# Grouped attention scores of the last two layers: two 64-row float32 products a block replaced by four 128-row float32r products, and the query norm moved behind the scores

## The reference

```python
def gqa_axial_attention(q, k, v, qn_g, kn_g, tables):
    q = rmsnorm_2(q.reshape(b, s, H_B, HEAD_DIM), qn_g)      # 8 query heads of 64
    k = rmsnorm_2(k.reshape(b, s, KV_HEADS, HEAD_DIM), kn_g) # 2 key heads of 64
    q = apply_axial_rope(q, tables)
    k = apply_axial_rope(k, tables)
    scale = HEAD_DIM ** -0.5
    ...
        sc = jnp.einsum('bqkgd,bskd->bkgqs', qblk, k) * scale
        p = jax.nn.softmax(sc, axis=-1)
        return jnp.einsum('bkgqs,bskd->bqkgd', p, v)

for l in range(2):
    h = rmsnorm_2(x, pre_g[l])
    u_a, v_a, g_a, q, k, v, g_b = split(h @ w_in[l])
    y_a = gmlp_group(u_a, layernorm(v_a), ...) * silu(g_a)
    y_b = gqa_axial_attention(q, k, v, ...) * silu(g_b)
    x = x + rmsnorm_2(concat(y_a, y_b) @ w_out[l], post_g[l])
```

## Time and profile before

| | |
|---|---|
| profiled execution | 1713.68 us, of it the span 1711.9 us |
| runs | 1713.58, 1709.22, 1713.06 us (median 1713.06) |
| granted TensorE clock | 0.993 over the span |
| PE busy | 97% of the span |
| DVE, ACT, POOL busy | 50%, 43%, 41% |
| chain that ended last | PE 86%, DVE 7%, ACT 4%, issue 2% |
| layer 1 of the second block | about 1206 to 1460 us |
| layer 2 of the second block | about 1460 to 1712 us |

### The profile page before, as it was taken

How to read it: one execution, slowest core, us unless ns; L and a number is a source line. 1 busy time by engine, 2 the same in 40 slices (tenths; PEclk the granted TensorE clock), 3 DMA queues, 4 the chain that set the end, 5 groups by cost and what they waited for, 6 DMA issues and landing times.

```text
span 1711.9 us, 24057 instructions
## 1 busy us (share of the span) xinstructions
PE 1663.8 (97%) x8728; PEld 1283.7 (75%) x8728; DVE 849.4 (50%) x1352; ACT 744.7 (43%) x1177; POOL 706.1 (41%) x406
## 2 busy tenths in 40 slices
PE   7899899999999999999999999999999999999998
PEld 7555678888888876666788888888876668876666
DVE  6787546555431125334466666411446454556354
ACT  6433434444432325444455555433326643526541
POOL 4433243444455444443534444554424423434332
PEclk9999999999999999999999999999999999999999
DMA  7112132333333332111323333333421112311111
GB/s 253 57 50 63 50 99 74 98 98 98 98 108 101 103 94 74 50 51 37 100 85 98 98 98 97 107 103 99 129 62 50 51 61 64 124 53 52 60 50 62
DMA packets 40251, 143.77 MB, mean 84 GB/s; under 512 B 4592, under 2 KB 4592, under 8 KB 40176
## 3 DMA queue, kind: packets, MB, share of 16 engines
q1 hardware_dynamic: 39168, 139.59, 26.6%
q10 hardware_dynamic: 1008, 3.15, 0.6%
HBM read 140.62 MB, written 2.10 MB: 83 GB/s over the span
## 4 chain that ended last, share of the span: by engine, by line
PE 86%; DVE 7%; ACT 4%; issue 2%; DMA 0%; POOL 0%; DVEq 0%; SPq 0%; ACTq 0%; POOLq 0%
PE banks L1686 23%; PE banks L1688 22%; PE banks L1687 22%; PE banks L1899 3%; PE banks L1864 3%; PE banks L1882 2%; PE banks L1732 2%; PE banks L1734 2%; PE banks L1733 2%; PE banks L1952 1%; ACT prob L723 1%; DVE chain L1373 1%; DVE nmax L1204 1%; DVE xs_lo L1165 1%; PE banks L2172 1%
## 5 line engine op out<-in xcount | busy, mean ns | idle before, releaser
L579 POOL TENSOR_TENSOR w_lo<-raw,w_hi 128x1024 fp32r<-128x1024 f32 x252 | 610.2, 2430 | 763.1 <-ACT w_hi L662 762.8
L1686 PE MATMUL banks<-xs_hi,w_hi 128*128 128x512 f32 (+2 forms) x1488 | 600.0, 403 | 10.3 <-DVE xs_lo L1424 4.2
L1688 PE MATMUL banks<-xs_hi,w_lo 128*128 128x512 f32 (+2 forms) x1488 | 579.2, 389 | 0.0
L1687 PE MATMUL banks<-xs_lo,w_hi 128*128 128x512 f32 (+2 forms) x1488 | 578.7, 389 | 0.0
L662 ACT ACTIVATE w_hi<-raw 128x1024 fp32r<-128x1024 f32 x255 | 263.9, 1053 | 295.0 <-PE banks L1688 257.1
L1686 PEld LDWEIGHTS banks<-xs_hi,w_hi 128*128 128x128 f32 x1488 | 281.0, 189 | 83.4 <-issue 18.9
L1688 PEld LDWEIGHTS banks<-xs_hi,w_lo 128*128 128x128 f32 x1488 | 280.9, 189 | 58.9
L1687 PEld LDWEIGHTS banks<-xs_lo,w_hi 128*128 128x128 f32 x1488 | 281.6, 189 | 53.2 <-issue 2.9
L589 POOL TENSOR_SCALAR prob<-prob,rinv 128x512 f32<-128x512 f32 (+3 forms) x144 | 88.7, 628 | 184.8 <-DVE rinv L1213 184.5
L723 ACT ACTIVATE prob<-banks,nmax 128x512 f32<-128x512 f32 (+3 forms) x144 | 83.2, 582 | 170.5 <-DVE nmax L1204 170.3
L1687 PE MATMUL banks<-hid_lo,w_hi 128*128 128x512 f32 x352 | 136.9, 389 | 0.0
(11 more groups left out here) (250 smaller groups left out, 1900.5 us busy)
## 6 DMA issues: line engine op xcount, KB each, us to landing
raw<-wstream SPq DMA_DIRECT2D x255, 512.0 KB, 3.6
x<-xT SPq DMA_DIRECT2D x4, 512.0 KB, 10.1
out<-pt SPq DMA_DIRECT2D x8, 256.0 KB, 2.0
memx<-memT SPq DMA_DIRECT2D x2, 512.0 KB, 7.0
ws_sb<-wsT ACTq DMA_DIRECT2D x2, 512.0 KB, 4.4
qk<-post_rows ACTq DMA_DIRECT2D x2, 512.0 KB, 3.8
sb_sb<-sbT ACTq DMA_DIRECT2D x2, 256.0 KB, 5.1
rope_sb<-rope ACTq DMA_DIRECT2D x1, 512.0 KB, 6.9
```

Of the source, the lines that this page charges most:

```text
L579: nc.gpsimd.tensor_tensor(w_lo[s][:].rearrange("p k c -> p (k c)"), raw[s][:], w_hi[s][:].rearrange("p k c -> p (k c)").bitcast(f32), SUB) ...
L1686: MM(dst, w_hi[slot][:, k, :], hi, start=start, stop=False)
L1687: MM(dst, w_hi[slot][:, k, :], lo, start=False, stop=False)
L1688: return MM(dst, w_lo[slot][:, k, :], hi, start=False, stop=stop)
```

## The change

In both layers of the second block:

1. **Scores.** `q_stack` holds, for each head of a pair, the float32r rounding of the query on one half of the partitions and the remainder on the other half. `k_hi` holds the rounded key of a head on both halves, `k_lo` its remainder on both halves. Each head's scores are two 128-row float32r products, `q_stack` by `k_hi` and `q_stack` by `k_lo` (four for a block), in place of one 64-row float32 product a head.
2. **Splits.** ACT makes the rounded parts (`q_high`: two 64x512 copies a pair, at units 6, 10, 13, 16; `k_high`: four at unit 7). DVE makes the remainders (`q_low`: two 64x512 subtractions a pair, at the same units; `k_low`: four at unit 8).
3. **Norm.** Only the key tile is cast and multiplied (`key_cast`, `key_norm`, at unit 7). The roots of the queries stay in `head_r`, times 64^-0.5, and are used as row factors: as `scale` of the exponentials, and by two 128x1 products behind the maximum.
4. **Silu.** The tiles of `gb` are done two at a time at units 12 and 16, those of `ga` two at unit 20 and one at unit 21.
5. **Turning x.** `x_turn` uses two banks in turn.
6. **Tables.** `k_lo` lies on the rope table, which is therefore loaded again in layer 2 (512 KB).

```diff
@@ attention on ACT
+                    kw = {"scale": head_r[:, 2 * i + e:2 * i + e + 1]} if a.scale_rows else {}
                     A(prob[b % 2][:, e, 0:nk], a.s[b % len(a.s)][:, e, 0:nk], ACT.Exp, bias=nmax[:, n:n + 1],
-                      accum_out=rsum[:, n:n + 1]).then_inc(at_exp, 1)
+                      accum_out=rsum[:, n:n + 1], **kw).then_inc(at_exp, 1)
@@ layer loop on ACT
-                if l == 0:
-                    act.dma_start(rope_sb[:], rope).then_inc(l2_in, 16)
+                act.dma_start(rope_sb[:], rope).then_inc(l2_in, 16)
...
+                def q_high(p):
+                    act.wait_ge(rope_ok, 5 * l + p + 1)
+                    if p == 1:
+                        act.wait_ge(rope_ok, 5 * (l + 1))
+                        act.wait_ge(qk_lo, 12 * l + 2)
+                    if p >= 2:
+                        act.wait_ge(at_s, 2 * (a.i0 + QT * (p - 1)))
+                    for e in range(2):
+                        A(q_stack[p % 2][e][half(e), :], qk[half(e), p, :], ACT.Copy).then_inc(qk_hi, 1)
+
+                def k_high():
+                    act.wait_ge(cast_down, cast_no[f"qk{l}"] + 1)
+                    for e in range(2):
+                        for h in range(2):
+                            A(k_hi[half(h), e, :], qk[half(e), 4, :], ACT.Copy).then_inc(qk_hi, 1)
...
+                    if j == 6:
+                        q_high(0)
+                    if j == 7:
+                        k_high()
+                    if j in (10, 13, 16):
+                        q_high((j - 7) // 3)
...
-                    if 11 <= j < 15:
-                        A(gb[:, j - 11, :], gb[:, j - 11, :], ACT.Silu).then_inc(gb_silu, 1)
-                    if j >= 19:
-                        A(ga[:, (j - 19) % 2, :], ga[:, (j - 19) % 2, :], ACT.Silu).then_inc(ga_silu, 1)
+                    if j in (12, 16):
+                        for t in (0, 1) if j == 12 else (2, 3):
+                            A(gb[:, t, :], gb[:, t, :], ACT.Silu).then_inc(gb_silu, 1)
+                    if j >= 20:
+                        for t in (0, 1) if j == 20 else (2,):
+                            A(ga[:, t % 2, :], ga[:, t % 2, :], ACT.Silu).then_inc(ga_silu, 1)
@@ DVE, the roots
+                if name[:2] == "qk":
+                    dve.wait_ge(stat_inv, n + 1)
+                    V.tensor_scalar(r[:, 0:8 * QT], r[:, 0:8 * QT], HD ** -0.5, None, MUL).then_inc(head_scale, 1)
@@ DVE, maxima
+                    own.link(V.tensor_reduce(nraw[:], scores_of, AX.X, ALU.max, negate=True))
+                    V.tensor_scalar(nmax[:, n:n + 1], nraw[:, 0:1], head_r[:, 2 * i:2 * i + 1], None, MUL)
+                    V.tensor_scalar(nmax[:, n + 1:n + 2], nraw[:, 1:2], head_r[:, 2 * i + 1:2 * i + 2], None,
+                                    MUL).then_inc(at_max, 1)
@@ layer loop on DVE
+                def key_norm():
+                    dve.wait_ge(rope_ok, 5 * (l + 1))
+                    dve.wait_ge(cast_up, cast_no[f"qk{l}"] + 1)
+                    V.tensor_tensor(qk[:, 4, :], qk[:, 4, :], cast_bank(f"qk{l}")[:], MUL).then_inc(cast_down, 1)
+
+                def q_low(p):
+                    dve.wait_ge(qk_hi, 12 * l + (2 if p == 0 else 6 + 2 * p))
+                    for e in range(2):
+                        V.tensor_tensor(q_stack[p % 2][e][half(1 - e), :], qk[half(e), p, :],
+                                        q_stack[p % 2][e][half(e), :].bitcast(f32), SUB).then_inc(qk_lo, 1)
+
+                def k_low():
+                    dve.wait_ge(qk_hi, 12 * l + 6)
+                    for e in range(2):
+                        for h in range(2):
+                            V.tensor_tensor(k_lo[half(h), e, :], qk[half(e), 4, :], k_hi[half(e), e, :].bitcast(f32),
+                                            SUB).then_inc(qk_lo, 1)
...
                     if j == 6:
                         rope(3)
                         invert(f"qk{l}")
+                        q_low(0)
+                    if j in (10, 13, 16):
+                        q_low((j - 7) // 3)
+                    if j == 8:
+                        k_low()
                     if j == 7:
                         rope(4)
-                        head_norm(0)
-                        head_norm(1)
-                    if j == 8:
-                        head_norm(2)
-                        head_norm(3)
+                        key_norm()
@@ PE
+                if a.stacked:
+                    for e in range(2):
+                        q = q_stack[p % 2][e][:, qt * P:(qt + 1) * P]
+                        MM(dst[:, e, :], q, k_hi[:, e, :], start=True, stop=False)
+                        MM(dst[:, e, :], q, k_lo[:, e, :], start=False, stop=True).then_inc(at_s, 1)
+                    return
...
-                    7: [(2, keys_up), (5, lambda: head_casts(0)), (7, lambda: head_casts(1))],
-                    8: [(2, lambda: head_casts(2)), (4, lambda: head_casts(3)), (7, lambda: head_casts(4))],
+                    7: [(2, keys_up), (5, lambda: key_cast())],
...
                 def x_turn(k):
-                    if k == 0:
-                        pe.wait_ge(cast_down, cast_no["pre0"] + 1)
+                    if k < 2:
+                        pe.wait_ge(cast_down, c0 + 1)
                     else:
-                        pe.wait_ge(xt_down, k)
+                        pe.wait_ge(xt_down, k - 1)
...
-                            pe.wait_ge(cast_down, c0 + 2 + i // QT)
+                            pe.wait_ge(qk_lo, 12 * l + 6 + 2 * (i // QT))
```

More of the change, by code:

```diff
@@ L177, in two_blocks @@
         sq_sum = put("sq_sum", [P, T], f32)
+        cursor[0] += (xs_at - cursor[0]) % LINE
         mem_kv1_at = cursor[0]
+        k_hi = put("k_hi", [P, 2, T], f32r, mem_kv1_at)
         mem_kv1 = put("mem_kv1", [P, 4, TM], f32)
@@ L183, in two_blocks @@
         small_t = put("small_t", [P, 64], f32)
+        head_r = put("head_r", [P, 40], f32)
+        nraw = put("nraw", [P, 2], f32)
         nmax = put("nmax", [P, 4], f32)
@@ L258, in two_blocks @@
         take = region()
+        q_stack = [[put("q_stack10", [P, T], f32r, take.at())]]
         qk = take("qk", [P, 5, T])
@@ L263, in two_blocks @@
         ua = take("ua", [P, AT, T])
+        q_stack.insert(0, [put(f"q_stack0{e}", [P, T], f32r, take.at() + e * T * 4) for e in range(2)])
         ga = take("ga", [P, 2, T])
@@ L270, in two_blocks @@
         sb_sb = take("sb_sb", [P, AT, P])
+        k_lo = put("k_lo", [P, 2, T], f32r, take.at())
         rope_sb = take("rope_sb", [P, 2, T])
+        q_stack[1].append(put("q_stack11", [P, T], f32r, take.at()))
         roped = take("roped", [P, T])
@@ L287, in two_blocks @@
         b_mix = bank[7]
+        b_turn = [bank[7], bank[6]]
         tight = ([two_banks[0], two_banks[2]], bank[6:8], bank[2:4])
@@ L390, in two_blocks @@
         rope_ok = sem("rope_ok")
+        head_scale = sem("head_scale")
+        qk_hi = sem("qk_hi")
+        qk_lo = sem("qk_lo")
         ga_silu = sem("ga_silu")
@@ L424, in attention @@
             a.p0 = sum(b.heads // 2 for b in attentions)
-            a.read = read
+            a.read, a.scale_rows, a.stacked = read, False, False
             attentions.append(a)
@@ L461, in two_blocks @@
             lambda p, l=l: (yb_ok, AT * l + p + 1), spaced) for l in range(2)]
+        for a in att_g:
+            a.scale_rows = True
+            a.stacked = True
         def keys_of(a, qt):
@@ L513, in two_blocks, with cast_bank @@
             cast_no[name] = count
-            count += 5 if name[:2] == "qk" else 1
-        QK_ORDER = (4, 0, 1, 2, 3)
-        def cast_bank(name, nth=0):
-            if name[:2] == "qk":
-                return bank[6 - nth % 2]
+            count += 1
+        def cast_bank(name):
             return b_mix if name in ("ln0", "ln1") else bank[5] if name == "pre0" else bank[6]
@@ L1134, in invert @@
                 m, t = (b_mix[:, TM + 64 * i:TM + 64 * i + w] for i in range(2))
-                r = small[:, 0:w]
+                r = (head_r if name[:2] == "qk" else small)[:, 0:w]
                 sums = b_mix[:, 0:w] if name != "pre1" else x_ss[:]
@@ L1532, in rope @@
                     V.tensor_tensor(qk[:, t, :], qk[:, t, :], roped[:], ADD).then_inc(rope_ok, 1)
-                def head_norm(nth):
-                    t = QK_ORDER[nth]
-                    dve.wait_ge(rope_ok, 5 * l + t + 1)
-                    dve.wait_ge(cast_up, cast_no[f"qk{l}"] + nth + 1)
-                    V.scalar_tensor_tensor(out=qk[:, t, :], in0=qk[:, t, :], scalar=HD ** -0.5 if t < 4 else 1.0,
-                                           in1=cast_bank(f"qk{l}", nth)[:], op0=MUL, op1=MUL).then_inc(cast_down, 1)
+                def key_norm():
[13 more added lines that the diff above has]
+                                            SUB).then_inc(qk_lo, 1)
                 def gated(p):
@@ L1577, in _ @@
                             maxima(a, i)
-                        if j == 9 and n == 0:
```

(12 more changed lines are left out.)

20 lines of the change are left out of this document (7 added, 13 removed).

## The result

The changed kernel took 1714.22 us (median of 11 runs, 1712.13 to 1717.08) against 1710.54 us (11 runs, 1709.04 to 1713.72) of the kernel before on the same chip: ratio 1.0021, 95% interval 1.0012 to 1.0031. The forecast was 1706. By the bound of 0.3% this is no change, on the slow side: the 7 us to be won did not come.

A forecast was written before the change was run, and what follows sets the result against it. PE, busy 97% of the span, was taken as the bound, with the softmax chain only 1 to 2 us ahead; 1713.7 - 20.6 saved + 13.4 added = 1706.5, taken as 1706; range 1696 to 1716, its own 1700 to 1712.

The forecast's parts named there:

- The saved side: PE in both layers: casts 9.6, score steps 8.1, waits that go 2.9; 20.6 us saved.
- the sum of what is added: New waits of PE: 2 x (0.6 + 1.7 + 3.9 + 0.3) + 0.4 = 13.4 us.
- Wait 3.6, and 0.3 for POOL: 3.9 a layer: Block 8: PE waits 3.6 us for block 7's exponentials, then 0.3 for POOL.
- Block 4: PE waits 1.4 us for block 3's exponentials and 0.3 for POOL; 1.7 a layer.
- block 12: ACT gets q_high(3), table loads and two silus, mostly in idle time; 0.3 us a layer (0 to 1.5).
- total_va: Unit 10: PE comes earlier and the partial sum on DVE later; 0.6 us more wait a layer.
- first scores: PE waits for k_low, 8.1 us behind the key's cast with POOL in between; 0.4 once (0 to 3).
- Block 8's mechanism: q_low(2) delays the layer norm's products, POOL's subtraction gets in first; products 4.0 us later.
- the cover holds: Rival: DVE and ACT chains have more slack than found, all 20.6 us come through; 1693, chance 0.17.
- stacked scores worth nothing: Rival: the new scores save PE nothing, by the row-group rule; 8.1 us less saved, 1714, chance 0.13.
- DVE becomes the bound: Rival: POOL catches each pair of subtractions, 11.6 us more; 1718, chance 0.15; decides from new waits over 10.3 a layer.
- The silus' 2.0: Block 9: PE's wait of 1.0 us in each layer goes, with no silu left at unit 14.

The follow-up runs named there:

- e4: Kernel before, with seven more copies of the layer norm's root on DVE at unit 13, both layers, to lengthen block 8's wait; 1724.8 us, ratio 1.0072.
- e11: Kernel before, with four more copies of the layer norm's root on DVE at unit 13, both layers; 1720.3 us, ratio 1.0044.
- e3: Changed kernel with the old float32 scores and no splits of q and k; row scales stay; 1707.2 us, ratio 0.9966.
- e1: Changed kernel with only pair 2's q_high and q_low moved into block 6's gap; 1712.4 us, ratio 0.9994.
- e12: Changed kernel with unit 14's weight copy behind block 7's exponentials and its POOL subtraction behind block 7's scaling; 1709.1 us, ratio 0.9979.
- e9: Changed kernel with all three pairs' splits in gaps, and unit 14's weight copy and POOL subtraction behind block 7's exponentials and scaling; 1695.7 us, ratio 0.9906.
- e10: Changed kernel with e9's moves, one 128x2 product behind each maximum, the partial sum's first additions in block 1's gap, k_low at unit 7; 1691.1 us, ratio 0.9877.
- e13: e10 with the old scores and no splits of q and k; 1697.5 us, ratio 0.9924.
- e7: Kernel before with only the silus regrouped as in the changed kernel; 1712.8 us, ratio 1.0001.
- e8: e10 but with POOL's old order, unit 14's subtraction ahead of block 7's scaling; 1702.4 us, ratio 0.9952.

## Why the prediction was wrong

- **The saved side held.** 25.3 lost and 3.5 longer make 21.8 saved, and PE's rows give the same: casts 9.7 (9.6 booked; 1.22 for each that stands alone), the steps of the scores 8.8 (8.1 booked; a plain step 2.09 before and 1.78 to 1.80 now), waits that went 3.2 (2.9 booked). 20.6 was booked in all.
- **The step that failed is the sum of what is added (13.4 booked, 25.3 measured), and in it first that a wait of PE was booked at its own length, its clock at nothing.** "Wait 3.6, and 0.3 for POOL: 3.9 a layer" is what block 8's wait is by its starts (4.2), but PE comes out of it at half clock, and that makes 4.5 us more, the largest missing term. The other 7.4 of the 11.9 missing are the waits below. The trap is set for the kernel before too (e4, e11), and its trace warned of it. Between the blocks no wait is over 1 us, but in the first part of the program the waits of 2.19 and 2.15 us have half clock beside them (clock 0.72 from 54 to 60 us, 0.57 from 76 to 80), and the prediction did not use them:

```profile
54.00 0.70 PE L1864 MATMUL banks<-mem_kv,qm 64*128 64x256 f32 x4 [2.19 <-ACT prob L723]
75.54 0.70 PE L1864 MATMUL banks<-mem_kv,qm 64*128 64x256 f32 x4 [2.15 <-ACT prob L723]
...
54.00:60.00 6.00, 5.61 (x20) 4.02 (x20) 5.24 (x11) 1.29 (x5) 2.67 (x4) 0.72 0.11 40
76.00:80.00 4.00, 4.00 (x15) 1.00 (x12) 2.66 (x5) 1.02 (x4) 0.87 (x2) 0.57 0.01 4
```

- The Trainium skill, "TensorE: Matmul & The Clock Gate", Part 1, "What's actually happening", says that PE's clock follows how busy it has lately been and is half when it has been idle. The traces here agree in direction: 0.50 behind waits, in old and new scores, though not behind every wait of 2 to 3 us.
- **Waits mis-sized, 7.4 in all.** Block 4 2.7 a layer for 1.7; block 12 1.0 for 0.3; total_va 1.0 for 0.6; block 8 4.2 for 3.9; first scores 1.2 for 0.4; blocks 5 and 15 not seen. One cause bears on blocks 4, 5, 8 and 12 and on total_va: the chain of a block grew by 0.54 and not by 0.3, the rest being the scaled exponentials. At total_va e3 shows it by itself (0.55 more wait with the old scores); the other 0.4 are PE coming earlier. A DVE addition met POOL there (2.76 for 0.7), but it did so before as well (2.74), so that is no new cost:

```profile
1289.03 2.74 DVE L1300 TENSOR_TENSOR sq_qk<-sq_qk,va 128x512 f32<-128x512 f32 x1
```

At the first scores k_low met POOL (4.92 for 2.8 alone), which the prediction had in its 8.1. How the rest of each wait divides was not measured.
- **Block 8's mechanism held**, to 0.3 us: `q_low(2)`, then POOL ahead of the products. It is shown by e1 and e12, each of which takes 1.5 of the 4.0 away, and by e9, where with both 0.38 is left.
- **Rival "the cover holds" (1693)** did not come, but it was right that the cover exists: DVE's idle time is there in every block, only not where the change puts its work. e9 and e10 reach 1695.7 and 1691.1.
- **Rival "stacked scores worth nothing" is refuted** by e10 and e13 (5.4 us in the stretch), and by the 1.78 to 1.80 for 2.09 of every plain step without a wait. The rule on row groups that spoke for it does not decide here: the side-by-side heads took 1.06 and the switches around them were real.
- **Rival "DVE becomes the bound"** had the sign right and the reason half: POOL met k_low and the partial sum (this one before too), but not `q_low(1)` or `q_low(3)`, and it was the clock that carried what was lost past the saved side: 12.7 a layer with it and 10.4 without, where 10.9 were saved (its own point was 10.3).
- The silus' 2.0 counted as a saving were, alone, a shift from block 9 to block 8 (e7).

What stays open: what decides whether a wait of 2 to 3 us is followed by half clock. 2.11 at block 4 was (e1, layer 2) and was not (the changed kernel, both layers), and e8 has 3.27 with full clock in layer 1 and half clock in layer 2. Why the clock of the work ahead of the layers differs from one execution to the next was not looked into either.
